# Where the modulation blocks of two layers are spread over a fused kernel's steps, and which queue reloads x

## The reference

```python
mod = c_act @ w_ada[l] + b_ada[l]                       # (1, 6144): shift, scale, gate
h = _rmsnorm(x, norm_g[l]) * (1.0 + scale[:, None, :]) + shift[:, None, :]
z = h @ w_in[l]                                         # 13 pieces of 512
...
y = jnp.concatenate([o_fft, o_na, o_ret, o_cv], axis=-1) @ w_out[l]
x = x + gate[:, None, :] * y
```

## Time and profile before

| | us |
|---|---|
| three timed runs | 2317.91, 2319.39, 2325.23 |
| median | 2319.39 |
| the profiled execution, its own time | 2315.48 |
| its span, first to last instruction | 2313.7 |
| TensorE busy | 2200.3 |
| VectorE busy | 1482.2 |
| ScalarE busy | 965.4 |
| DMA queue of SyncE / of GpSimd, share of 16 engines | 38.3% / 26.4% |
| mean granted TensorE clock | 0.98 |

### The profile page before, as it was taken

How to read it: one execution, slowest core, us unless ns; L and a number is a source line. 1 busy time by engine, 2 the same in 40 slices (tenths; PEclk the granted TensorE clock), 3 DMA queues, 4 the chain that set the end, 5 groups by cost and what they waited for, 6 DMA issues and landing times.

```text
span 2313.7 us, 33056 instructions
## 1 busy us (share of the span) xinstructions
PE 2200.3 (95%) x13686; PEld 1830.5 (79%) x13686; DVE 1482.2 (64%) x1904; ACT 965.4 (42%) x1337; POOL 203.3 (9%) x388
## 2 busy tenths in 40 slices
PE   5979899998899999998999999999999999999998
PEld 3768777886697877886777787888777989988876
DVE  0445667876674677874688656576976778554554
ACT  2324544553443554554642222223436544344443
POOL 2210110111011010101001000010100010000000
PEclk8989999999999999999999999999999999999999
DMA  9988576777679767667567545563866598522253
GB/s 359 401 261 287 202 259 204 254 256 288 229 245 292 247 243 248 232 209 287 186 230 237 164 146 180 157 192 127 276 244 225 180 303 267 166 65 73 69 191 136
DMA packets 225454, 509.84 MB, mean 220 GB/s; under 512 B 36064, under 2 KB 40288, under 8 KB 222752
## 3 DMA queue, kind: packets, MB, share of 16 engines
q1 hardware_dynamic: 170048, 298.39, 38.3%
q0 software_dynamic: 55120, 209.08, 26.4%
q10 hardware_dynamic: 144, 0.36, 0.0%
HBM read 499.38 MB, written 8.39 MB: 219 GB/s over the span
## 4 chain that ended last, share of the span: by engine, by line
PE 72%; DMA 11%; DVE 10%; ACT 4%; issue 2%; POOL 0%; SPq 0%; DVEq 0%; ACTq 0%; POOLq 0%
PE ps L769 20%; PE ps L770 20%; PE ps L771 20%; DMA w_raw<-in_w_in 6%; DVE ada_acc L2151 3%; PE ps L825 3%; DMA ada_raw<-in_ada_w 2%; DVE wl L2238 1%; DMA w_raw<-in_w_out 1%; PE ps L1430 1%; ACT wh L1534 1%; DVE wl L2231 1%; DMA rsw<-in_ada_w 1%; PE ps L953 1%; PE ps L966 1%
## 5 line engine op out<-in xcount | busy, mean ns | idle before, releaser
L2238 DVE TENSOR_TENSOR wl<-w_raw,wh 128x1024 fp32r<-128x1024 f32 x280 | 335.3, 1223 | 267.2 <-ACT wh L1534 266.2
L1534 ACT ACTIVATE wh<-w_raw 128x1024 fp32r<-128x1024 f32 x280 | 291.7, 1056 | 439.3 <-PE ps L771 263.4
L1587 ACT ACTIVATE wh<-w_raw 128x1024 fp32r<-128x1024 f32 x220 | 230.6, 1058 | 444.2 <-PE ps L771 388.9
L769 PE MATMUL ps<-hh,wh 128*128 128x256 f32 x1280 | 375.2, 293 | 7.3 <-DVE hl L2291 7.0
L2231 DVE TENSOR_TENSOR wl<-w_raw,wh 128x1024 fp32r<-128x1024 f32 x220 | 266.5, 1221 | 179.3 <-ACT wh L1587 179.0
L770 PE MATMUL ps<-hh,wl 128*128 128x256 f32 x1280 | 364.1, 284 | 0.0
L771 PE MATMUL ps<-hl,wh 128*128 128x256 f32 x1280 | 363.4, 284 | 0.0
L2151 DVE SCALAR_TENSOR_TENSOR ada_acc<-ada_raw,cpad,ada_acc 128x1024 f32<-128x1024 f32 x264 | 330.9, 1281 | 26.0 <-DMA ada_raw<-in_ada_w 23.9
L769 PEld LDWEIGHTS ps<-hh,wh 128*128 128x128 f32 x1280 | 245.8, 192 | 31.6 <-issue 20.2
L769 PE MATMUL ps<-wh,act_hl 128*128 128x512 f32 x640 | 257.4, 402 | 6.4 <-DVE wl L2231 6.4
L770 PE MATMUL ps<-wh,act_hl 128*128 128x512 f32 x640 | 253.8, 397 | 0.0
(11 more groups left out here) (377 smaller groups left out, 3419.4 us busy)
## 6 DMA issues: line engine op xcount, KB each, us to landing
ada_raw<-in_ada_w POOLq DMA_DIRECT2D x272, 512.0 KB, 5.2
w_raw<-in_w_in SPq DMA_DIRECT2D x208, 512.0 KB, 6.4
w_raw<-in_pool_in SPq DMA_DIRECT2D x72, 512.0 KB, 4.5
w_raw<-in_w_out SPq DMA_DIRECT2D x64, 512.0 KB, 5.6
w_raw<-in_mla_in SPq DMA_DIRECT2D x56, 512.0 KB, 4.7
ada_fourth<-in_ada_w POOLq DMA_DIRECT2D x48, 512.0 KB, 6.2
w_raw<-in_pool_out SPq DMA_DIRECT2D x48, 512.0 KB, 5.0
w_raw<-in_mla_out SPq DMA_DIRECT2D x32, 512.0 KB, 4.2
```

The costliest lines, as they stand in the source:

```text
L769: pe.matmul(dst, ah, bh, start=start, stop=False, skip_group_check=True)
L1534: act.activation(wh[:, g % RING, :], w_raw[:, g % RING, :], ACT.Copy).then_inc(w_hi, 1)
L1587: act.activation(wh[:, r, :], w_raw[:, r, :], ACT.Copy).then_inc(w_hi, 1)
L2238: dve.tensor_tensor(wl[:, g % RING, :], w_raw[:, g % RING, :], wh[:, g % RING, :].bitcast(F32), ALU.subtract).then_inc(w_lo, 1)
```

## The change

The diff has five parts.

1. The tables ADA_DVE and ADA_PE are drawn up anew, with the same number of blocks on each engine. In layer 0, VectorE now has 1 block in steps 0 to 7, 2 in 8 to 11, 1 in 12 to 15, 2 in 16 to 26, then 1, 0, 2, 1, 1, 1 in 27 to 32; TensorE has 1, 1, 2, 2, 2, 2, 3, 3 in steps 3 to 10 instead of 2 each. In layer 1 VectorE has 1 in steps 0 to 3 and 2 in 4 to 9; TensorE has 1, 2, 2, 2, 3, 3, 3 in steps 2 to 8 and 3, 3, 2, 2, 3, 3 in 26 to 31.
2. VectorE does its blocks of steps 8 to 25 directly behind the four subtractions of the step (ADA_AHEAD), ahead of the pieces and the mixers, and from step 26 on at the end of the step, behind the products, the subtractions o_lo, the gate's diagonal row and the residual.
3. TensorE's blocks of a step with fewer than three stay ahead of the third slot. With three or more, the first two go ahead of the second slot and the others ahead of the fourth. 20 steps have three or more: 9, 10 and 12 to 16 of layer 0, and 6, 7, 8, 11 to 14, 18, 19, 26, 27, 30 and 31 of layer 1.
4. The reload of x in each layer is issued by ScalarE in step 28, between its second and third rounding, behind the same wait for o_lo. GpSimd keeps the context load of layer 1, with a wait for the products (small_mul) alone. The last reload of x is issued by SyncE behind slot 15 of the last projection.
5. The slab loads of layer 1 are one behind each of the slots 4 to 19 (steps 1 to 4). In the first group of the pooling layer 5 blocks are behind the slots of u and 11 behind those of gate, instead of 8 and 8.

```diff
--- before.py
+++ after.py
@@ -55,7 +55,7 @@
 ADA_RING_A = 4
 ADA_EARLY = 4 * KT
 EARLY_RING = 8
-SLAB_AT = 5 * RING
+SLAB_SLOTS = ({g: 2 for g in range(20, 28)}, {g: 1 for g in range(4, 20)})
 X_OUT_AT = ((0, 0, 31 * RING), (0, 1, 33 * RING), (1, 2, 0), (1, 3, 2 * RING))
 EARLY_PIECES = (0, 2, 1, 3)
 
@@ -97,15 +97,17 @@
     return out
 
 
-ADA_DVE = [{**spread(0, 0, [1] * 16), **spread(1, 17, [1, 1] + [2] * 7), **spread(3, 26, [2] * 8)},
-           {**spread(0, 0, [2] * 6 + [1] * 4), **spread(1, 10, [1] * 14 + [2])}]
-ADA_PE = [{**spread(2, 3, [2] * 8), **spread(4, 12, [4] + [3] * 4), **spread(5, 19, [2] * 8)},
-          {**spread(2, 2, [2] * 5 + [3] * 2), **spread(3, 11, [3] * 4 + [2] * 2), **spread(4, 18, [3] * 2 + [2] * 5),
-           **spread(5, 26, [3] * 4 + [2] * 2)}]
+ADA_DVE = [{**spread(0, 0, [1] * 8 + [2] * 4), **spread(1, 12, [1] * 4 + [2] * 6),
+            **spread(3, 22, [2] * 5 + [1, 0, 2, 1, 1, 1])},
+           {**spread(0, 0, [1] * 4 + [2] * 6), **spread(1, 10, [1] * 14 + [2])}]
+ADA_PE = [{**spread(2, 3, [1, 1, 2, 2, 2, 2, 3, 3]), **spread(4, 12, [4] + [3] * 4), **spread(5, 19, [2] * 8)},
+          {**spread(2, 2, [1, 2, 2, 2, 3, 3, 3]), **spread(3, 11, [3] * 4 + [2] * 2), **spread(4, 18, [3] * 2 + [2] * 5),
+           **spread(5, 26, [3, 3, 2, 2, 3, 3])}]
 ADA_FIN = [{11: 2, 17: 4, 18: 0, 27: 5, 28: 1, 34: 3}, {9: 2, 10: 0, 17: 3, 25: 4, 28: 1, 32: 5}]
 ADA_SUMMED = [(0, 1, 3), (0, 1)]
 ADA_BANKS = [7 if t <= 17 else 5 for t in range(STEPS)]
 ADA_FIN_BANKS = [ADA_BANKS, [4 if t == 28 else b for t, b in enumerate(ADA_BANKS)]]
+ADA_AHEAD = range(8, SMALL_STEP)
 CTX_SSQ, CTX_VAR = OUT_STEP + 2, OUT_STEP + 4
 CTX_TURN = {(5, 0): 0, (5, 1): 1, (5, 3): 2, (6, 0): 3, (6, 2): 4, (6, 3): 5, (7, 1): 6, (7, 2): 7}
 
@@ -132,7 +134,7 @@
 
 
 ADA_SEQ, ADA_DONE = ada_schedule()
-X_BACK_AT = [min(i for i, x in enumerate(ADA_SEQ) if x[0] == l and x[1] > OUT_STEP) for l in range(DEPTH)]
+CTX_AT_ = min(i for i, x in enumerate(ADA_SEQ) if x[0] == 1 and x[1] > OUT_STEP)
 
 
 assert len(ADA_SEQ) % ADA_RING_A == 0
@@ -175,7 +177,8 @@
 MLA_SCALE = float((NOPE + ROPE) ** -0.5)
 
 POOL_STAGES = [("ctx", 0, 8, 0)]
-POOL_STAGES += [s for g in range(4) for s in (("u", g, 8, 8), ("gate", g, 8, 8), ("grp", g, 2, 0))]
+POOL_STAGES += [s for g in range(4) for s in (("u", g, 8, 8 if g else (0, 0, 0, 1, 1, 1, 1, 1)),
+                                              ("gate", g, 8, 8 if g else (1, 1, 1, 1, 1, 2, 2, 2)), ("grp", g, 2, 0))]
 AHEAD = 10
 POOL_STAGES += [("out", 0, 8, (0, 0, 0, 2, 2, 2, 2, 2)), ("out", 1, 8, (2, 2, 2, 0, 2, 2, 1, 1)),
                 ("octx", 2, 8, (0, 0, 0, 0, 1, 0, 1, 0)), ("octx", 3, 8, (1, 0, 1, 0, 1, 0, 1, 0)),
@@ -610,14 +613,15 @@
                     sp.wait_ge(w_lo, l * SLOTS_A + g + 1)
                     sp.dma_start(w_raw[:, g % RING, :].rearrange("p (k n) -> p k n", k=SLOT_K), src
                                  ).then_inc(w_landed[g % RING], 16)
-                    if g == SLAB_AT:
+                    if g == min(SLAB_SLOTS[l]):
                         if l:
                             sp.wait_ge(small_mul, 4 * l)
                         else:
                             sp.wait_ge(h_lo, 8)
-                    if SLAB_AT <= g < SLAB_AT + HEADS:
-                        slab_load(l, g - SLAB_AT, 0)
-                        slab_load(l, g - SLAB_AT, 1)
+                    if g in SLAB_SLOTS[l]:
+                        first = sum(n for at_, n in SLAB_SLOTS[l].items() if at_ < g)
+                        for i in range(first, first + SLAB_SLOTS[l][g]):
+                            slab_load(l, i // 2, i % 2)
                     for layer, q, after in X_OUT_AT:
                         if (layer, after) == (l, g):
                             a = slice(q * GRP, (q + 1) * GRP)
@@ -675,6 +679,10 @@
                 for s in range(BLK):
                     load(g, mout[:, SLOT_K * s:SLOT_K * s + SLOT_K, q * GRP:(q + 1) * GRP])
                     g += 1
+                    if q == 1 and s == BLK - 1:
+                        sp.wait_ge(p_olo, 16)
+                        sp.wait_ge(stored, 32)
+                        sp.dma_start(x4[:, 0:TT, :], save_t).then_inc(x_back, 16)
             for q in range(4):
                 sp.wait_ge(t_add, 16 + 2 * q + 2)
                 a = slice(q * GRP, (q + 1) * GRP)
@@ -729,16 +737,9 @@
                 for q, (layer, t, j, k, _, _) in enumerate(ADA_SEQ):
                     if layer != l:
                         continue
-                    if q == X_BACK_AT[l]:
-
-                        pool.wait_ge(o_lo, l * 8 + 8)
-                        if l:
-                            pool.wait_ge(x_saved, 64 * l)
-                        pool.dma_start(x2, save_t if l else x.rearrange("(t p) n -> p t n", p=P)
-                                       ).then_inc(x_back, 16)
-                        if l:
-                            pool.wait_ge(small_mul, 4 * DEPTH)
-                            pool.dma_start(x4[:, TT:AT, :], ctx_v).then_inc(b_in, 16)
+                    if l and q == CTX_AT_:
+                        pool.wait_ge(small_mul, 4 * DEPTH)
+                        pool.dma_start(x4[:, TT:AT, :], ctx_v).then_inc(b_in, 16)
                     lay, kind, half = ada_piece(l, j)
                     ada_load(q, lay, 2 * kind + half, k)
 
@@ -757,10 +758,7 @@
                     pool.dma_start(save_v, x4[:, 0:TT, :]).then_inc(stored, 16)
                 ada_load_more(i)
 
-            pool.wait_ge(p_olo, 16)
             pool.wait_ge(stored, 32)
-            pool.dma_start(x4[:, 0:TT, :], save_v).then_inc(x_back, 16)
-            pool.wait_ge(x_back, 16 * DEPTH + 16)
 
         @block.tensor
         def _(pe):
@@ -995,12 +993,17 @@
                             pe.wait_ge(small_mul, l * 4 + 4)
                         ada_sum(ADA_SUMMED[l].index(j) % 2, 0, ADA_FIN_BANKS[l][t])
 
-                def ada_middle(t):
-
-                    if t in ADA_FIN[l]:
+                def ada_middle(t, i):
+
+                    if i == 2 and t in ADA_FIN[l]:
                         ada_turn(ada_event(l, t), ADA_FIN_BANKS[l][t])
+                    here = sum(x[4] and x[0:2] == (l, t) for x in ADA_SEQ)
+                    seen = 0
                     for q, (layer, step, j, k, by_pe, _) in enumerate(ADA_SEQ):
                         if by_pe and (layer, step) == (l, t):
+                            seen += 1
+                            if i != (2 if here < 3 else 1 if seen < 3 and t not in ADA_FIN[l] else 3):
+                                continue
                             if k == 0:
                                 pe.wait_ge(ada_read, max([4 + 6 * l] + [ada_event(l, x) + 1 for x in ADA_FIN[l] if x < t]))
                             pe.wait_ge(*ada_here(q))
@@ -1013,8 +1016,8 @@
                         g = t * RING + i
                         p, s = SLOTS_OF[l][g]
                         bank0 = 4 if l == 0 and p == 2 else 2 * (p % 2)
-                        if i == 2:
-                            ada_middle(t)
+                        if i:
+                            ada_middle(t, i)
                         if p == 0:
                             pe.wait_ge(h_lo, l * 8 + s + 1)
                             if l and s == 0:
@@ -1037,8 +1040,9 @@
                     m, s = i // 2, i % 2
                     if i == 0:
                         pe.wait_ge(ft_lo, l * NCH + NCH)
+                    if i:
+                        ada_middle(SMALL_STEP, i)
                     if i == 2:
-                        ada_middle(SMALL_STEP)
                         pe.wait_ge(cv_lo, l + 1)
                         pe.wait_ge(rt_var, l * 4 + 4)
                     slot(g, l * SLOTS_A + g, True, 4 if m else 2, SLOT_K * s, s == 0, s == 1,
@@ -1084,8 +1088,8 @@
                                 row_of(4 * l + 2 * q + 1)
                         if l and (2 * q + i // RING, i % RING) in CTX_TURN:
                             turn_ctx(CTX_TURN[2 * q + i // RING, i % RING])
-                        if i % RING == 2:
-                            ada_middle(OUT_STEP + 2 * q + i // RING)
+                        if i % RING:
+                            ada_middle(OUT_STEP + 2 * q + i // RING, i % RING)
                         if q == 0:
                             pe.wait_ge(o_lo, l * 8 + i + 1)
                         slot(g, l * SLOTS_A + g, False, 2 * (q % 2), SLOT_K * s, i == 0, i == BLK - 1, hh, hl)
@@ -1741,6 +1745,13 @@
                         his(t, base, l * STEPS, (2,))
                         ctx_h(5)
                         his(t, base, l * STEPS, (3,))
+                    elif t == OUT_STEP + 1:
+                        his(t, base, l * STEPS, (0, 1))
+                        act.wait_ge(o_lo, l * 8 + 8)
+                        if l:
+                            act.wait_ge(x_saved, 64 * l)
+                        act.dma_start(x2, (x_save if l else x).rearrange("(t p) n -> p t n", p=P)).then_inc(x_back, 16)
```

(8 more changed lines are left out.)

## The result

The changed kernel takes 2280.77 us (median of 4 runs, 2278.85 to 2282.14) against 2318.65 us (median of 4, 2317.79 to 2325.23) beside it: a ratio of 0.9835, 95% interval [0.9813, 0.9857]. Forecast were 2278. Its profiled execution took 2281.84 us with a span of 2280.2; the profiled execution of before took 33.6 us more.

What follows compares the result with a forecast made beforehand. TensorE, busy 95% of the span, was taken as the bound, its waits and half clock as winnable: 57.6 us gross less 4.8, 7.0, 2.0 and 3.0 leaves 40.8; 2315.5 - 41 = 2274.5, plus 3.9: 2278 us, 8 in 10 within 2266 to 2300.

Steps and rivals of the forecast that it cites:

- the likeliest case: Whole kernel: 2278 us, chance 0.60, own range 2268 to 2290.
- The clock: Six stretches of TensorE at half clock, 37.4 us in all, cost 18.7 us more, counted as winnable.
- Step 12 of layer 0: TensorE's 8.64 us wait for its fourth block goes wholly, as VectorE's block stands right behind the subtraction; bound 2 us stay.
- Late subtractions: Layer 0: 9.0 us of waits for weight rests, largest 5.46 at step 30, and 1.6 for the diagonal row nearly all go.
- Layer 1, steps 4 to 8: Waits of 4.2 us and 5.1 of clock go with the slab move; 7.0 us come new in steps 6 and 7.
- Step 28 of layer 1: Block waits of 5.6 us and 5.1 of clock, behind x and context in GpSimd's queue, go except 1 us.
- Pooling layer: At its start all 6.6 us of TensorE's waits for weight rests go; bound 2 us stay.
- Visits: A second place for TensorE's blocks in 20 steps costs 0.24 us each, 4.8 us in all.
- (a): Ring of four takes the gain back: eight block waits of 2.4 us give 19 more, 2297 us; chance 0.17.
- (b): x on its own queue starves the weights in both layers' reloads: 14 us less gain, 2292 us; chance 0.13.
- (d): Slower: VectorE's blocks of steps 8 to 25, ahead of the mixers, wait for late loads; 2331 us, chance 0.05.

Runs made afterwards that it cites:

- u1: Changed kernel with all of TensorE's blocks of a step in one place again, ahead of the third slot; 2286.07 us.
- u2: Changed kernel with VectorE's blocks of steps 8 to 25 behind the mixers again; 2293.74 us.
- d2: Changed kernel with the old table of blocks and VectorE's blocks of steps 26 to 34 ahead of the residual again; 2283.48 us.
- u3: Changed kernel with all three reloads of x in GpSimd's queue again; 2283.08 us.
- u4: Changed kernel with layer 1's sixteen slab loads two to a slot again, at slots 20 to 27; 2290.92 us.
- u6: Changed kernel with the old table of which step takes which blocks (ADA_DVE, ADA_PE), places, order and queues kept; 2280.03 us.
- d1: Changed kernel with x reloaded in four quarters of 512 KB, each later one behind the residual of the quarter before; 2274.91 us.
- u5: Changed kernel with the modulation blocks of the pooling layer's first group one to every slot again; 2289.79 us.
- b1: Changed kernel with two places only in five-block steps, layer 1's context load later, x in quarters, VectorE's step 25 blocks of layer 0 inside the LayerNorm; 2269.6 us.

## Why the prediction came out right, and where it did not

The time was 2.8 us above the forecast, inside the likeliest case's own range. By the profiled executions 41 us were forecast and 33.6 came. That the total came nearer than that is luck: the forecast adds the 3.9 us by which the median of before lay above its profiled execution, and the median of the changed kernel lies 1.1 below its own. The steps, in the prediction's order:

- **The clock: a term that was too large.** Half the length of the six stretches at half clock was taken, 18.7 us. But TensorE was busy for only 28.2 of their 37.4 us (the sum line of the earlier trace rows); the rest was waiting, which the sum already held. Half of 28.2 is 14.1, so 4.6 us were counted twice. Taken this way step 12 comes out to the tenth: 8.64 of wait and 3.57 / 2 of clock, less 0.33 for its second place, make 10.1, and the step went from 26.70 to 16.59. Step 30 of layer 0 does too: TensorE was busy for 5.00 us of its stretch, 5.46 + 2.50 = 7.96, and the step went from 19.17 to 11.20.
- **Step 12 of layer 0: right.** 26.7 us became 16.6, the pause and its half clock are gone, and the load of the fourth block landed 8.5 us behind the step's start (273.3 against 264.8), as 277.6 against 268.4 had said to within 0.7. u1 and u2 show that the order did it.
- **Late subtractions: right in size but for step 26, partly wrong in their reasons.** Steps 15 went by the order of the blocks, as u2 shows. The 5.5 us pause and the diagonal row's wait are gone too. I had explained the first by 2.56 us of order and 2.56 us of an earlier reload. By d2 the order is worth 1.0 us there. The block's load behind x, which I had put last, is what every variant without the pause has lost; no run restores that load alone, so this is inferred. The weights of step 29 were late there as well: the last landed 20.2 us behind the end of step 27 before, 14.3 in u3 and 11.4 in the changed kernel. Step 26 kept 1.4 of its 1.6 us: a block ahead of a serial chain costs what it costs behind it. I had read VectorE's idle time of the step and not asked whether it lies before or behind the place of the block.
- **Layer 1, steps 4 to 8: off in place, the size not shown.** A gain of 4.2 + 5.1 - 7.0 = 2.3 us was forecast, and 2.7 came in this execution; others of the same program took as long as the kernel before. 7.0 us of new waits and clock were forecast in steps 6 and 7; 2.4 us came in step 5, 0.6 at the start of step 5, 0.6 in step 7 and 1.7 us of clock, 5.3 in all. The slab move is worth 10 us with the new table (u4), more than the 9.3 us that I had seen in the rows of before; the new table fills the steps that the slabs had stood in, and u4's three pauses are there.
- **Step 28 of layer 1: the step that failed.** Forecast were 5.6 + 5.1 us less 1, that is 9.7. The step did fall from 23.9 to 15.6 us, and step 30 rose from 14.1 to 20.8: the stage won 1.2 us. The 8.5 us missing here (1.5 of them the clock's double count) are more than the whole difference of 7.4 between the 41 us forecast and the 33.6. In the kernel before the fourth weights of step 29 landed 19.2 us behind step 27 too, but TensorE then still stood in step 28, which ended at 23.9. The pause had hidden the shortage that caused it. "What is late next" was left unasked for this stall. The residual stands on VectorE behind that fourth subtraction, the roundings of step 30 behind the residual. What took the gain is the new table: with the old one the stage wins 8.5 us (u6, d2). u3 shows that moving x to ScalarE's queue neither caused nor cured the shortage here, d1 that fewer bytes in shorter rows ease it.
- **Pooling layer: right.** 8.8 us against 8.3; u5 gives back 9.0.
- **Visits: the term was mis-sized.** 0.33 us each and not 0.24, 6.6 us instead of 4.8. I had counted the gap between the matmuls on either side, and that is 0.22 here too; a step's length has 0.1 us more. The Trainium skill, TensorEngine Tiling (Array Packing), section on tiling modes (key properties), says that a change of the tiling mode drains the engine; 0.33 us for going in and out once more agree with it; the page gives no figure.
- **Rivals.** (a) did not come: blocks' waits behind step 7 are 4.2 us in both layers. (b) had the right place, late weights in the reload of layer 1, and its turns are seen in the packets (0.38 MB of weights in 7 us with three queues at work, 0.54 with two), but the step from there to later weights failed: they land at the same time in u3. Its sign, weights landing above 13 us, was badly chosen: loads of step 29 of layer 1 took 13.3 to 17.1 us, but 11.9 to 16.8 in the kernel before too, while those of layer 0 took under 10. The Trainium skill, DMA: Bandwidth & Descriptors, section on issuing engines not being separate queues, says that loads of all engines run on the same 16 DMA engines and that another issuer saves only its own time; u3 agrees in layer 1 (weights landed within 0.2 us of each other), but not in layer 0, where the last landed 2.9 us later in u3. (d) did not come: no wait of VectorE for blocks shows in steps 8 to 25.

Open stays why the same program takes 203.2 to 208.0 us up to step 7 of layer 0. In the 24 slots of MLA a large part is the clock: where they took 80.1 to 81.4 us (before, u6, d1, b1) no stretch there was granted half, where they took 82.1 to 84.6 one or two of 3.4 us were; why the one or the other comes isn't shown. Open is also how the old table spares steps 28 to 34 in u6, though it has three blocks in step 28. Its next block loads are asked for 11.1 us behind step 27 and not 8.3, and its last two weights of step 29 land at 14.0 and 15.4; from 12 to 14 us behind step 27 the weights moved 0.76 MB there, with GpSimd's queue all but empty, and 0.33 in the changed kernel. That fits with the bytes again, but was not tried by itself.

## What to carry to other kernels

When a pause is to go, read when the next stage's loads landed inside it, not only when they were wanted: a load that lands 19 us into a step which its pauses stretch to 24 is the next pause. Where transfers overlap, what is asked for (a quarter of x in short rows, a context later) did more here than who asks. Where TensorE waits inside a stretch at half clock, count the clock on its busy time alone. Move filler work into the wait itself, behind the last link of the chain that the wait closes; ahead of that chain it costs its full length.

## What the runs showed of the hardware

- A place of its own for 128x32 matmuls among 128x128 ones costs 0.33 us beyond the matmuls (16.15 against 15.83 in step 13 of layer 0).
- With the same program and no late load a step's length repeats to 0.04 us from one kernel's execution to another's; where loads are late, a stage scatters by 3 to 5 us.
- Three queues with work took turns packet for packet: 186, 194 and 186 packets in 7 us, of 8, 4 and 2 KB, so that x moved 1.47 MB and the weights 0.38.
- Moving a 2 MB load from GpSimd's queue to ScalarE's left the landing of four 512 KB loads on SyncE's queue where it was in layer 1, to 0.2 us, and brought the last of them forward by 2.9 us in layer 0; asking for 0.5 MB in rows of 2 KB instead of 2 MB in rows of 8 KB brought those of layer 1 forward by 2.3, 2.4, 4.5 and 6.4 us.
- The length of a pause alone does not tell whether half clock follows: in u1 a pause of 1.8 us in layer 1's first steps had 3.4 us of it behind, in u3 one of 2.2 us at 678.9 had none.
